# Retention's output projection, second head: seven half-size products per pair of output blocks, and a fixed place for the normalisation's sum matmul

## The reference, cut to what matters

```
def readout(o, g):
    n = o.shape[2]
    y = rms_norm_2(o).transpose(0, 2, 1, 3).reshape(B, n, hv).astype(g.dtype)
    return (jax.nn.silu(g) * y) @ w_out
```

## Time and profile before

| | |
|---|---|
| median of three runs | 2763.23 us |
| the profiled execution, its own time | 2761.79 us |
| its span | 2760.0 us |
| TensorE matmul busy | 2729.2 us (99%) |
| VectorE busy | 2026.0 us (73%) |
| ScalarE busy | 1292.1 us (47%) |
| GpSimd busy | 371.7 us (13%) |
| granted TensorE clock | 0.999 |

### The profile page before, as it was taken

The page is one execution under the profiler, slowest core; times in us unless marked ns, Lnnn a source line. Parts: engine busy times, 40 slices in busy tenths (PEclk is TensorE's granted clock), DMA queues, the critical chain, the costliest instruction groups (busy, mean ns, idle before and its releaser), DMA issues.

```text
span 2760.0 us, 43032 instructions
## 1 busy us (share of the span) xinstructions
PE 2729.2 (99%) x16362; PEld 2453.6 (89%) x16362; DVE 2026.0 (73%) x3735; ACT 1292.1 (47%) x2387; POOL 371.7 (13%) x206
## 2 busy tenths in 40 slices
PE   9999999999999999999999999999999999999998
PEld 8888896988888889998888999999997787989898
DVE  7788778868896827886966896567685536778686
ACT  6332348642233525555543743334356546545354
POOL 2343300023433010000101000000002323000000
PEclk9999999999999999999999999999999999999999
DMA  6565512236555343446451022222223121222322
GB/s 205 189 191 190 169 64 85 77 105 212 189 193 157 130 154 136 169 145 226 185 183 55 18 65 84 65 70 65 81 70 103 50 77 54 68 85 93 107 92 85
DMA packets 101725, 327.13 MB, mean 119 GB/s; under 512 B 10896, under 2 KB 24592, under 8 KB 99984
## 3 DMA queue, kind: packets, MB, share of 16 engines
q1 hardware_dynamic: 86688, 267.23, 30.2%
q10 hardware_dynamic: 14832, 57.15, 5.4%
HBM read 292.36 MB, written 30.41 MB: 117 GB/s over the span
## 4 chain that ended last, share of the span: by engine, by line
PE 90%; DVE 5%; ACT 2%; DMA 2%; issue 1%; ACTq 0%; POOL 0%; SPq 0%; DVEq 0%; POOLq 0%
PE ps L2248 28%; PE ps L2249 28%; PE ps L2250 28%; PE ps L2528 1%; PE ps L2512 1%; PE ps L2501 1%; DVE t_wlo L2984 1%; DMA t_raw<-in_gu 1%; DMA t_m<-in_dist 1%; PE ps L2392 0%; ACT t_whi L2571 0%; PE ps L2384 0%; PE ps L2443 0%; PE ps L2400 0%; DMA t_x<-in_x 0%
## 5 line engine op out<-in xcount | busy, mean ns | idle before, releaser
L2571 ACT CAST t_whi<-t_raw 128x512 fp32r<-128x512 f32 (+3 forms) x497 | 382.9, 780 | 543.3 <-PE ps L2250 343.0
L2248 PE MATMUL ps<-t_h,t_whi 128*128 128x256 f32 (+2 forms) x1832 | 617.0, 337 | 4.7 <-DVE t_tmp L3014 1.5
L2249 PE MATMUL ps<-t_h,t_wlo 128*128 128x256 f32 (+2 forms) x1832 | 612.7, 334 | 0.0
L2250 PE MATMUL ps<-t_h,t_whi 128*128 128x256 f32 (+2 forms) x1832 | 612.7, 334 | 0.0
L2984 DVE TENSOR_TENSOR t_wlo<-t_raw,t_whi 128x512 fp32r<-128x512 f32 (+2 forms) x424 | 356.0, 849 | 118.0 <-ACT t_whi L2571 114.1
L2248 PEld LDWEIGHTS ps<-t_h,t_whi 128*128 128x128 f32 x1832 | 346.8, 189 | 37.7 <-issue 9.2
L2250 PEld LDWEIGHTS ps<-t_h,t_whi 128*128 128x128 f32 x1832 | 346.8, 189 | 25.5
L2249 PEld LDWEIGHTS ps<-t_h,t_wlo 128*128 128x128 f32 x1832 | 346.9, 189 | 25.4 <-issue 0.2
L2248 PE MATMUL ps<-t_hid,t_whi 128*128 128x256 f32 (+2 forms) x1032 | 335.5, 325 | 0.6 <-DVE t_hid L3283 0.6
L2249 PE MATMUL ps<-t_hid,t_wlo 128*128 128x256 f32 (+2 forms) x1032 | 333.6, 323 | 0.0
L2250 PE MATMUL ps<-t_hid,t_whi 128*128 128x256 f32 (+2 forms) x1032 | 333.1, 323 | 0.0
(11 more groups left out here) (367 smaller groups left out, 4949.5 us busy)
## 6 DMA issues: line engine op xcount, KB each, us to landing
t_raw<-in_gu SPq DMA_DIRECT2D x174, 512.0 KB, 3.4
t_raw<-in_ada SPq DMA_DIRECT2D x96, 512.0 KB, 3.7
t_raw<-in_dn SPq DMA_DIRECT2D x52, 512.0 KB, 3.9
s_v<-t_hid ACTq DMA_DIRECT2D x24, 512.0 KB, 3.3
t_h<-s_v ACTq DMA_DIRECT2D x24, 512.0 KB, 6.7
t_raw<-in_dn SPq DMA_DIRECT2D x24, 384.0 KB, 3.5
s_qk<-t_hid ACTq DMA_DIRECT2D x12, 768.0 KB, 6.8
t_raw<-in_ret_v SPq DMA_DIRECT2D x16, 512.0 KB, 3.7
```

What stands on the lines that cost most here:

```text
L2248: e.matmul(out, whi, xlo, start=first, stop=False, skip_group_check=shared)
L2249: e.matmul(out, wlo, xhi, start=False, stop=False, skip_group_check=shared)
L2250: return e.matmul(out, whi, xhi, start=False, stop=last, skip_group_check=shared)
L2571: e.copy(m.block(0, it.slot, n), m.raw(it)).then_inc(*S["hi"].of(j))
```

## The change

1. `TURNED = (1,)`: for head 1 `output` calls `small_products`. Each pair j2 is a 2 x 2 problem: two blocks of 128 columns, two halves of the 512 channels (k of 0, 1 and k of 2, 3) and two halves of the 768 tokens (384 each). Seven products of two k steps and 384 tokens stand for it. The weights' pieces (256 elements a partition) are A11, A12, A22 and the sums S1 to S4; the tokens' are B11, B21, B22 and the sums T1 to T4.
2. `out_add` adds each product straight to x once for every quarter of the result that it belongs to, 12 instructions a pair. Some products follow others in the same bank without clearing it (P6 and P7 on P1's, P3 on P5's, P4 on P1's for the first three pairs).
3. Weights: seven casts of 256 elements, seven low parts of 256 on GpSimd, four sums (`small_sum`) of 256 on VectorE for each pair, in half slots.
4. Activations: T1 to T4 for two k (`y_sum`), high parts (`y_hi`, ScalarE) and low parts (`y_lo`), 384 wide; k = 0 on VectorE, k = 1 on GpSimd.
5. `ret_finish` leaves `FLOATING`. The context tokens' is issued after value step (0, 2), not (0, 1). The latent tokens' (`latents`) is issued for heads 0 and 2 in the next head's `attend`, ahead of value step (512, 1), and for heads 1 and 3 after the first pair of the output that runs then.

```
-    FLOATING = (... "ret_finish",
+    FLOATING = (... "v_turn",
...
+                if h and (t0, i) == (512, 1) and h - 1 not in TURNED:
+                    latents(h - 1)
                 put("ret_value", h=h, t0=t0, n=n, i=i, kt=kt, at=at, last=last, before=before)
...
-                if (t0, i) == (0, 1):
+                if (t0, i) == (0, 2):
                     finish(h, 512, 256)
...
+        def latents(h):
             finish(h, 0, 512)
             gated_values(h, 0, 512)
+            if h in TURNED:
+                turned_values(h)
...
+        def small_products(h, between):
+            for j2 in range(4):
+                banks = {"P1": bank(), "P2": bank(), "P5": bank()}
+                banks.update(P6=banks["P1"], P7=banks["P1"], P4=banks["P2" if j2 == 3 else "P1"], P3=banks["P5"])
...
+                p1 = product("P1", "A11", "B11", leaves("P1", ...))
+                a1 = add("P1", p1, 0, 0)
+                p5 = product("P5", "S1", "T1", leaves("P5", ("P3", 384), ("P3", 512)))
+                a5 = add("P5", p5, 1, 1)
+                p2 = product("P2", "A12", "B21", leaves("P2", ("P2" if j2 < 3 else "P4", 0)))
+                a2 = add("P2", p2, 0, 0)
+                p6 = product("P6", "S2", "T2", a1)
+                a6 = add("P6", p6, 0, 1)
+                while waiting:
+                    waiting.pop()()
+                p3 = product("P3", "S4", "B22", a5)
+                add("P3", p3, 0, 1)
+                if j2 == 3:
+                    add("P4", product("P4", "A22", "T4", a2), 1, 0)
+                p7 = product("P7", "S3", "T3", a6)
+                a7 = add("P7", p7, 1, 1)
...
+            if h:
+                once = [h] if h == n_head - 1 or h in TURNED else []
+                done = output(h - 1, lambda: latents(once.pop()) if once else None)
...
+    def out_add(it):
+        e.scalar_tensor_tensor(out=x, in0=m.PS[:, it.bank, o:o + it.n], scalar=m.mod(0, it.who, 2, it.j), in1=x,
+                               op0=ALU.mult, op1=ALU.add)
...
     def ret_split(it):
+        if h in TURNED:
+            w.wait_ge(f"ret_tsum{c % 2}", (h, "T4", c % 2))
```

More of the change, by code:

```diff
@@ L47 @@
 QUADS = ("A11", "S1", "S2", "S4", "S3", "A12", "A22")
+SMALL = ("A11", "S1", "A12", "S2", "S4", "S3", "A22")
 HALF = 20
@@ L533, in assign_half @@
         (pid, srcs), q = known[j]
+        if srcs[0] == "ret_o":
+            low[j] = "lo_pool"
+            if q == "A11":
+                put("load", pid=pid, which=0, src=srcs, small=True)
+            if q == "A11":
+                for name in ("S3", "S1"):
+                    put("small_sum", pid=pid, q=name, after=[])
+            if q in ("S2", "S4"):
+                put("small_sum", pid=pid, q=q, slot=slot, after=after)
+            put("prep", j=j, slot=slot, after=after, lo=low[j], q=q, pid=pid, small=True)
+            if q == "S4":
+                put("prep_lo", j=j - 1)
+            if q != "S2":
+                put("prep_lo", j=j)
+            return
         low[j] = "lo_dve"
@@ new lines, in small_products, with product, add, leaves @@
+        def small_products(h, between):
+            waiting, last = [], None
+            for j2 in range(4):
+                if j2 == 1 and between:
+                    between()
+                key, ops = (h, j2), small_pair(j2, h)
+                banks = {"P1": bank(), "P2": bank(), "P5": bank()}
+                banks.update(P6=banks["P1"], P7=banks["P1"], P4=banks["P2" if j2 == 3 else "P1"], P3=banks["P5"])
+                def product(name, q, x, before, key=key, ops=ops, banks=banks, j2=j2):
+                    j = ops[q]
+                    ready(j)
+                    g = put("seven", w=j, slot=where[j], lo=low[j], name=name, f="out", ver=h, x=x, n=384, bank=banks[name],
+                            first=name in ("P1", "P2", "P5") or name == "P4" and j2 == 3, before=before)
+                    tick(2 * 416 / 800)
+                    over(j, "ps", g.id)
+                    return g.id
+                def add(name, g, row, col, key=key, banks=banks, j2=j2):
+                    j = j2 * 2 + row
+                    for t0, n in (((0, 384),), ((384, 128), (512, 256)))[col]:
+                        cell = (row, col, t0)
+                        before = [("drain_dve", ("l00", h - 1, j, s)) for s in range(t0 // 256, -(-(t0 + n) // 256))]
+                        if h - 1 in TURNED:
+                            before = [added[h - 1, j, col, t0]]
+                        it = put("out_add", key=(*key, name, t0), g=g, bank=banks[name], j=j, who=int(t0 >= 512), t0=t0, n=n,
+                                 x=[added[key, cell]] if (key, cell) in added else before)
+                        added[key, cell] = ("out_add", it.key)
+                        added[h, j, col, t0] = ("out_add", it.key)
+                    return [("out_add", (*key, name, t0)) for t0, _ in (((0, 384),), ((384, 128), (512, 256)))[col]]
+                def leaves(name, *adds, key=key, banks=banks):
+                    before = owner.get(banks[name], [])
+                    owner[banks[name]] = [("out_add", (*key, *a)) for a in adds]
+                    return before
+                p1 = product("P1", "A11", "B11", leaves("P1", *(("P4", 0),) if j2 < 3 else (("P7", 0), ("P7", 384), ("P7", 512))))
+                a1 = add("P1", p1, 0, 0)
[13 more added lines that the diff above has]
+                a7 = add("P7", p7, 1, 1)
+                if j2 == 3:
+                    add("P7", p7, 1, 0)
+                    last = p7
+                    break
+                def rest(product=product, add=add, a7=a7):
+                    nonlocal last
+                    last = product("P4", "A22", "T4", a7)
+                    add("P4", last, 1, 0)
+                waiting.append(rest)
+                if not known:
+                    waiting.pop()()
+            while waiting:
+                waiting.pop()()
+            turn_free[0] = [("ps", last)]
+            return ("ps", last)
@@ L1535, in output @@
+        def output(h, between=None):
             chain = lambda s: layer_norm_chain(
                 s, "l00", 0, lambda c, s: [("drain_dve", ("l00", 3, c, s))], after_ln("l00", 5, 0, 0, 3), True)
-            post = gated("l00", 0, 2, 3, chain, lambda j, s: [("x_alpha", (j, s))])
+            post = gated("l00", 0, 2, 3, chain, lambda j, s: [("x_alpha", (j, s))],
+                         lambda j, t0, n: [added[h - 1, j, col, a] for col, a, b in ((0, 0, 384), (1, 384, 512), (1, 512, 768)) if a < t0 + n and t0 < b])
+            if h in TURNED:
+                return small_products(h, between)
@@ L1841, in schedule @@
             loads.append(it)
-        if it.kind == "load":
+        if it.kind == "load" and "small" in it:
+            raws[it.pid, 0] = it.raw
+            it["last"] = [(it.pid + SMALL.index(q), "lo_pool") for q in ("S4", "S3", "A12", "S1", "A22")]
+            it["shape"] = (2, 512)
+        elif it.kind == "load":
             raws[it.pid, it.which] = it.raw
             it["last"] = [(it.pid + QUADS.index(q), low[it.pid + QUADS.index(q)]) for q in (("S4", "S3", "A12"), ("S1", "S2", "A22"))[it.which]]
+        if it.kind == "small_sum":
+            it["raw"] = raws[it.pid, 0]
+            it["slots"] = {q: where[it.pid + SMALL.index(q)] for q in ("S2", "S4")}
         if it.kind == "wadd":
```

169 lines of the change are left out of this document (147 added, 22 removed).

## The result

The changed kernel takes 2775.94 us (median of five runs, 2772.33 to 2776.71), the kernel before 2763.37 beside it; the ratio is 1.0039, 95% interval 1.0028 to 1.0051. Instead of 3.65 us faster it is 12.6 us slower, outside the forecast's range. The profiled execution took 2772.33 us, 10.5 more than that of before, with a span of 2770.5.

A forecast was written before the change was run, and what follows sets the result against it. TensorE's instruction stream plus its stalls bounds the kernel (busy 2729.2 of 2760.0 us). Terms -4.2 - 3.0 + 2.1 + 0.25 + 0.3 + 0.7 + 0.2 = -3.65 from 2763.23 give 2759.6 us, range 2755.5 to 2764.0.

The forecast's parts named there:

- Columns, -4.2: In output(1), 168 matmuls of 384 columns at 0.173 us take 29.1 us instead of 33.3: 4.2 us less on TensorE.
- The wait of 3.0 goes: TensorE's 3.0 us wait in output(1) for head 2's sum of squares disappears, as that sum moves to attend(3): -3.0 us.
- Head 0's fixed place, +2.1: In attend(1), head 0's latent sum, now ahead of value step (512, 1), waits for its operand: 1.6 to 2.5 us, taken as 2.1.
- rival (a): Head 0's fixed place costs nothing, the due time bringing the squares forward, and output(1) runs clean: -6.4, 2756.8 us; chance 0.29.
- The context sums move later by a value step: 0.: The four context sums, issued one value step later in the heads' attention, were to cost nothing.
- T sums, +0.2 (0 to 1): T1 to T4 work fits in attend(2); a GpSimd part of 1 us may hold up a score's low part: 0.2 us.
- output(1), +0.7 with 0 to 10: VectorE, GpSimd and ScalarE in output(1): weight sums waiting for GpSimd make a few products late, 0.7 us; between 0 and 10.
- banks +0.25 and +0.3: PSUM bank hand-overs: 0.25 us at the start of output(2), 0.3 us (0 to 0.6) at the second score of attend(3).
- the upper bound: In output(1), each of a pair's 16 VectorE instructions waits for GpSimd; the period is 9.8 instead of 7.3, four pairs lose 10 us.
- the forecast's 4.2 us a pair: VectorE time for a pair's additions in output(1): three of 384 columns and four times 128 + 256, 1.6 + 2.6 us.
- the tight link: In output(1), the first pair's P7 waits for P6's two additions, 0.95 us, covered by one product, P3, for 1.04.
- Rival (c): In output(1), the removed columns come back wholly as waits of P6, P3 and P7 on additions, 3 us: 2762.6 at most; chance 0.15.

The follow-up runs named there:

- e4: The kernel before with only head 2's latent sum moved, fixed in attend(3) ahead of value step (512, 1); 2758.76 us, -3.8 from before.
- e6: e1 with head 0's latent sum floating again, all other sums fixed; 2762.73 us, 0.0 from the kernel before.
- e9: e6 with every head's context sum floating again too; 2760.46 us, -2.2 from the kernel before.
- e3: The changed kernel with all T sums and their low parts on VectorE, none on GpSimd; 2766.93 us, +4.4 from the kernel before.
- e8: The changed kernel with T work on VectorE and sums floating at old places, except head 2's latent sum fixed as in e4; 2764.34 us, +1.7 from before.
- e1: The changed kernel with head 1's output as before, so only the sums' places are changed; 2763.89 us, +1.4 from the kernel before.
- e2: The changed kernel with the sums' matmuls floating at their old places, seven products and T sums kept; 2770.09 us, +7.6 from the kernel before.
- e5: e1 with the context sums back behind value step (0, 1), still fixed; 2765.75 us, +3.1 from the kernel before.
- e11: e8 with only the first 64 columns of the distances loaded for heads 1 to 3; 2763.00 us, +0.3 from the kernel before.
- e12: The changed kernel with all T sums on VectorE, only the second block's four low parts left on GpSimd; 2769.71 us, +7.0 from the kernel before.
- e15: e4 with two 128x256 reciprocals on VectorE ahead of head 1's decay table; 2767.00 us, +4.7 from the kernel before.
- e14: e4 with one 128x256 reciprocal on VectorE ahead of head 1's decay table; 2758.87 us, -3.4 from the kernel before.
- e10: e6 with only the first 64 columns of the distances loaded for heads 1 to 3; 2761.25 us, -1.4 from the kernel before.

## Why the prediction was wrong

**Columns, -4.2: right.** In the changed kernel the matmuls of 384 columns run 0.173 apart; without its three waits the projection takes 32.5 - 2.4 = 30.1 us, against 29.1 by the term. The rest is some tenths at the start, where before has a gap too, and behind each wait, whose next distance is 0.25 and not 0.173.

**The wait of 3.0 goes: right.** No such row is left in the changed kernel, and e4 alone measured -3.8.

**Head 0's fixed place, +2.1: right in size, on another instruction, and too narrow.** The first latent sum itself never waits. The due time made the plan put the squares (ScalarE, ahead of the high parts of the next scores) first, as rival (a) had it, but that wasn't free: TensorE waits 2.07 us for a score's low part. By e6 that is +1.3 in the median, within the noise of two medians. What I put at 0 was the rest: "The context sums move later by a value step: 0." Fixing them let their reciprocal slip into the middle of the next decay table, +2.3 (e6 less e9). The traces have 1.98 us of waits and 1.8 of clock in e6 against 1.11 of waits in e9, so two thirds of it are the clock. I looked at what a fixed sum waits for, and not at what its due time moves on VectorE's list.

**T sums, +0.2 (0 to 1): this is the step that failed.** It measured 8 to 9 us for the part on GpSimd alone (changed kernel less e3); the trace has 10.4 us at that place, 7.1 of waits and 3.3 of clock. The prediction had both the row and the rule: a y multiply at 2.88 us for 0.69 beside GpSimd. I applied it to `output(1)`, where I expected 10 us at worst, and for the T sums I counted busy time: "VectorE busy for 20.19 of 30.1 us, so the work fits there". But the plan didn't put that work into `attend(2)`. It put it around the end of `output(0)` (VectorE from 1369.4 to 1382.1, GpSimd from 1373.3 to 1384.1, with TensorE's last matmul of the stage at 1380.87), where VectorE must also empty the banks that `attend(2)` starts in. There was no room there before the change either: VectorE was busy for 29.2 of the 30 us from 1350 to 1380, and had only the stretch behind it free (6.1 of 10 us). Busy us there in the changed kernel (TensorE, weight loads, VectorE, ScalarE, GpSimd, then the columns as above): VectorE is full.

```profile
1370.00:1385.00 15.00, 12.78 (x78) 11.04 (x76) 14.96 (x18) 6.52 (x16) 11.59 (x10) 1.00 0.00 1
```

My bound of 1 us took one GpSimd part against one low part. Eight on each engine, GpSimd's taking turns with whatever VectorE had on SBUF, are what stands ahead of the 7.1 us of waits and 3.3 us of clock. The Trainium skill, "SBUF — State Buffer", under "SBUF: two separate sides", has the shared port pair as an exclusive lock for a whole instruction, so that two queues which both need it can only go in turns. The trace agrees: VectorE's four low parts took 4.95 us while GpSimd worked without a break, and 1.96 us while it was idle.

**output(1), +0.7 with 0 to 10, and banks +0.25 and +0.3: low, but of the right kind.** The projection has 2.4 us of waits, and `attend(3)` has 0.59 where 0.3 was put; the gap of 0.25 at the start of `output(2)` is there (0.48 us ahead of 1485.10). The additions are 45, 11 a pair and 12 in the last, and not 12 in each, as the description of the change and the upper bound have it; the forecast's 4.2 us a pair are the sum of 11. The PSUM additions are not stretched, 0.61 us for 384 columns beside GpSimd and without it, as I had read from the earlier trace rows; what delayed them was SBUF-only work in front of them. The wait of 0.88 us is P7 of the first pair, the tight link; ahead of its addition a step of the decay table (L3710) took 0.82 us, where the four of before take 0.29 each. Ahead of the other two (0.37 and 1.19 us) stood a weight sum, which overwrites the raw weights in place and waited 0.71 and 1.48 us for GpSimd's low part:

```profile
1441.71 0.43 DVE L3172 TENSOR_TENSOR t_raw<-t_raw 128x256 f32<-128x256 f32 x1 [1.48 <-POOL t_wlo L3903]
1442.05 0.61 DVE L3218 SCALAR_TENSOR_TENSOR t_x<-ps,t_mod,t_x 128x384 f32<-128x384 f32 x1
```

Rival (c), columns given back as waits, is what e8 shows without GpSimd in the T sums, though larger than I had it: 9.6 us for 4.2 by the medians.

**What no term had: the clock.** It was 1.00 in every window I read, and I priced each wait at its length. In the changed kernel, e1, e2, e3, e5, e6, e8, e11, e12 and e15 waits of about 2 to 4 us were followed by some us at the lower level, 1.8 to 3.3 us over 30 us. Of each kernel one execution was profiled.

## What to carry to other kernels

Count a new elementwise operation at the place in the engine's list where it will stand, and not against the mean load of its stage; ahead of it look for what empties the banks that TensorE needs next. Splitting SBUF-to-SBUF work between VectorE and GpSimd gave nothing here where both ran at once, and took from VectorE what GpSimd used: eight operations moved back were worth 8 to 9 us. And before a scheme that saves columns is paid for with order changes, undo the parts one by one: one moved matmul gave all the gain there was (2758.8 us), while the rest, taken together, lost.

## What the runs showed of the hardware

- VectorE and GpSimd on SBUF operands took turns: four 128x384 low parts 1.96 us alone, 4.95 us while GpSimd worked without a break. An operation with one PSUM and one SBUF input was not slowed: of the changed kernel's 45 additions none took over 0.62 us.
- After a wait TensorE ran for a while at half its clock: in e8 matmuls of 384 columns 0.32 us apart behind a 3.08 us wait (granted clock 0.59 from 1418 to 1421), in e6 matmuls of 512 columns 0.43 us apart behind 1.98 us (0.54 from 1317.5 to 1320). It didn't follow every such wait: the changed kernel shows 1.00 from 1300 to 1330 with waits of 2.61 and 2.07 us, while e12, with waits of 2.64 and 2.08 us at the same place, shows 0.94. So the length of the waits alone doesn't decide it; what does stays open.
- A 448 KB transfer of distances landed 5.4 us after its issue before (5.4 to 5.6 in e4, e14 and e15), and 6.3 to 7.5 us in the changed kernel, e1, e3, e5, e6, e9 and e12, at the same point of the score sequence. With 32 KB in place of 448 it still took 5.3 us (e10). It wasn't tried what it shared the queues with.
